# Attention output: the value bank's two halves are summed by TensorE as they are turned back, and VectorE scales the sum

## The reference

```python
# branch A (latent attention), one block of queries
s = jnp.where(mask[None, None], s.astype(jnp.float32), NEG_INF)
p = jax.nn.softmax(s, axis=-1).astype(v_a.dtype)
return jnp.einsum('bhqk,bkhd->bqhd', p, v_a)
# branch B (sparse attention): top-k keys, a bias by distance, then the same softmax and product
p = jax.nn.softmax(s, axis=-1).astype(vs.dtype)
return jnp.einsum('bhqk,bqkhd->bqhd', p, vs)
```

## Time and profile before

| | before |
|---|---|
| median of 3 runs | 1461.71 us (1460.07 to 1461.95) |
| the profiled execution's own time | 1460.28 us |
| its span, first to last instruction | 1458.5 us |
| mean granted TensorE clock | 0.969 |
| PE / PEld busy | 93% / 77% |
| DVE / ACT / POOL busy | 69% / 45% / 31% |

### The profile page before, as it was taken

How to read it: one execution, slowest core, us unless ns; L and a number is a source line. 1 busy time by engine, 2 the same in 40 slices (tenths; PEclk the granted TensorE clock), 3 DMA queues, 4 the chain that set the end, 5 groups by cost and what they waited for, 6 DMA issues and landing times. The chain is left out here.

```text
span 1458.5 us, 21714 instructions
## 1 busy us (share of the span) xinstructions
PE 1361.1 (93%) x7307; PEld 1117.2 (77%) x7308; DVE 1007.6 (69%) x1891; ACT 659.6 (45%) x1175; POOL 459.2 (31%) x497
## 2 busy tenths in 40 slices
PE   6989999999999999999999979999859999999973
PEld 4779888888989978888777768899857776777741
DVE  5448999999970277777777754342387777777746
ACT  5348323321212146777777741121135666666622
POOL 1100335421215545555555214200112332333313
PEclk9999999999999999999999989999959999999996
DMA  6031543257432904868776255222279999999818
GB/s 213 30 143 40 185 161 111 88 197 228 134 101 100 246 1 80 187 134 225 210 206 179 68 178 159 86 89 87 73 281 389 348 366 351 356 379 372 344 58 326
DMA packets 106926, 273.76 MB, mean 188 GB/s; under 512 B 27393, under 2 KB 56737, under 8 KB 94425
## 3 DMA queue, kind: packets, MB, share of 16 engines
q1 hardware_dynamic: 92208, 229.20, 45.5%
q0 software_dynamic: 13584, 38.62, 10.4%
q10 hardware_dynamic: 1048, 4.82, 0.9%
HBM read 246.99 MB, written 85.96 MB: 228 GB/s over the span
## 5 line engine op out<-in xcount | busy, mean ns | idle before, releaser
L445 PE MATMUL ps<-hHi,g_lead 128*128 128x512 f32 (+2 forms) x480 | 184.5, 384 | 5.8 <-DVE hLo L877 3.6
L330 DVE TENSOR_SCALAR_CACHE_REDUCE mask<-score,cand 128x272 bf16<-128x272 f32 (+6 forms) x224 | 185.5, 892 | 4.6 <-DVE cand L349 4.4
L2364 DVE TENSOR_TENSOR w_rest<-wgu,w_lead 128x1024 fp32r<-128x1024 f32 x128 | 156.0, 1222 | 46.4 <-ACT w_lead L2309 45.2
L446 PE MATMUL ps<-hLo,g_lead 128*128 128x512 f32 (+2 forms) x480 | 183.9, 383 | 0.0
L447 PE MATMUL ps<-hHi,g_rest 128*128 128x512 f32 (+2 forms) x480 | 182.6, 380 | 0.0
L1382 DVE TENSOR_TENSOR pL<-ps,pH 128x512 fp32r<-128x512 f32 (+3 forms) x224 | 124.8, 573 | 56.8 <-ACT pH L1321 54.2
L2309 ACT CAST w_lead<-wgu 128x1024 fp32r<-128x1024 f32 x124 | 130.8, 1055 | 48.3 <-PE ps L2252 48.3
L762 POOL TENSOR_TENSOR g_rest<-g_raw,g_lead 128x2048 fp32r<-128x2048 f32 x12 | 56.7, 4722 | 298.4 <-ACT g_lead L619 298.4
L1321 ACT CAST pH<-ps 128x512 fp32r<-128x512 f32 (+3 forms) x224 | 106.0, 495 | 53.8 <-PE ps L1266 53.1
L2250 PE MATMUL ps<-w_lead,x_lead 128*128 128x512 f32 x256 | 114.5, 447 | 4.0 <-DVE x_rest L2371 4.0
L2272 PE MATMUL ps<-wd,hmT 128*128 128x512 f32 x256 | 115.3, 593 | 1.6 <-DVE hmT L2387 1.0
(11 more groups left out here) (382 smaller groups left out, 3414.3 us busy)
## 6 DMA issues: line engine op xcount, KB each, us to landing
wgu<-in_w_exp_gate SPq DMA_DIRECT2D x32, 1024.0 KB
wgu<-in_w_exp_up SPq DMA_DIRECT2D x32, 1024.0 KB
wd<-in_w_exp_down SPq DMA_DIRECT2D x32, 1024.0 KB, 11.8
bias_d<-mask_d POOLq DMA_DIRECT2D x8, 2368.0 KB, 15.6
g_raw<-in_w_in SPq DMA_DIRECT2D x16, 1024.0 KB, 7.2
gates_d<-stage SPq DMA_DIRECT2D x32, 256.0 KB, 2.0
gt<-gates_d SPq DMA_DIRECT2D x32, 256.0 KB, 3.1
tbm<-bias_d SPq DMA_DIRECT2D x8, 976.0 KB, 6.2
```

The source lines that it names most:

```text
L330: return dve.tensor_scalar(mask[:, OFF[i]:OFF[i + 1]], score[:, OFF[i]:OFF[i + 1]], thr, 0.0, op, ALU.add, accum_out=cnt[:, i:i + 1])
L445: pe.matmul(dst, x[0], y[0], start=(k == 0), stop=False)
L446: pe.matmul(dst, x[0], y[1], start=False, stop=False)
L2364: dve.tensor_tensor(w_rest[u][:, :, 2 * part:2 * part + 2, :], wgu[u][:, :, 2 * part:2 * part + 2, :], w_lead[part][:, :, :, :].bitcast(F3 ...
```

## The change

The four transposes of a q turn become four true float32 matmuls. The stationary operand is a block of `oT`, as it was, and the moving operand is a constant `fold` of 128x64: two identity matrices of 64 on top of each other. Each product is therefore 128 tokens by 64, the sum of both halves, and a q turn writes 256 columns of its bank, not 512. DVE's reduction into `otmp` goes; DVE multiplies the bank by `rec` straight into `otok`. POOL's scaling goes, with its place in POOL's order and its waits. `fold` is made once, early on, by one DVE addition of 128x64. The semaphore `s_qa` goes; the bank is free when `s_om` counts.

```diff
+        fold = keep("fold", VD)
@@ early, where the other small constants are made
                 dve.memset(onesb[:, :], 1.0).then_inc(s_cb, 1)
+                dve.tensor_tensor(fold[:, :], ident[:, 0:VD], ident[:, VD:2 * VD], ALU.add).then_inc(s_cb, 1)
@@ TensorE, emptied() and turn()
                     elif kind == "q":
-                        pe.wait_ge(s_qa, s + 1)
+                        pe.wait_ge(s_om, s + 1)
                         elif kind == "q":
-                            mm = pe.transpose(dst, oT[s % 2][:, P * b:P * (b + 1)], ident)
+                            mm = pe.matmul(bank[:, VD * b:VD * (b + 1)], oT[s % 2][:, P * b:P * (b + 1)], fold[:, :],
+                                           start=True, stop=True)
@@ VectorE
                     elif kind == "q":
                         dve.wait_ge(s_t, k + 1)
-                        if s >= 2:
-                            dve.wait_ge(s_om, s - 1)
-                        both = bank_of(k).rearrange("p (b l c) -> p b c l", b=4, l=2)
-                        dve.tensor_reduce(otmp[s % 2][:, :, :], both, AX.X, ALU.add).then_inc(s_qa, 1)
+                        dve.wait_ge(s_rc, s + 1)
+                        if s >= 4:
+                            dve.wait_ge(s_t, turn_of[("o", 4 * (s // 4) - 4 + 2 + s % 2, 0)] + 1)
+                        u, c = s // 2 % 2, 4 * (s % 4)
+                        dve.tensor_tensor(otok[s % 2][:, :].rearrange("p (b c) -> p b c", b=4)[:, :, VD * u:VD * (u + 1)],
+                                          bank_of(k)[:, 0:4 * VD].rearrange("p (b c) -> p b c", b=4),
+                                          rec[:, c:c + 4].unsqueeze(2).to_broadcast([P, 4, VD]),
+                                          ALU.mult).then_inc(s_om, 1)
@@ GpSimd
-                def scaled(s):
-                    ...
-                    if s >= 1:
-                        scaled(s - 1)
                     if s % 2 == 1 and s // 2 + 2 < H:
                         joined(pool, s // 2 + 2)
-                scaled(NSS - 1)
```

More of the change, by code:

```diff
@@ L1049, in hybrid_layer @@
         oT = [at(f"oT{k}", [P, 512], F32, R_X + 4096 * RING + 2048 * k) for k in range(2)]
-        otmp = [at(f"otmp{k}", [P, 4, VD], F32, R_S + 16384 + 1024 * k) for k in range(2)]
         OaT = at("OaT", [P, 4, T], F32, R_W)
@@ L1142, in bank_of @@
             return ps[:, bank_no[k], :]
-        (s_qk, s_ml, s_ex, s_t, s_ld, s_rs, s_pv, s_ot, s_qa, s_rc, s_om, s_oe, s_z, s_vz, s_hl, s_hr, s_vl,
-         s_vr) = map(sem, ["s_qk", "s_ml", "s_ex", "s_t", "s_ld", "s_rs", "s_pv", "s_ot", "s_qa", "s_rc",
+        (s_qk, s_ml, s_ex, s_t, s_ld, s_rs, s_pv, s_ot, s_rc, s_om, s_oe, s_z, s_vz, s_hl, s_hr, s_vl,
+         s_vr) = map(sem, ["s_qk", "s_ml", "s_ex", "s_t", "s_ld", "s_rs", "s_pv", "s_ot", "s_rc",
                            "s_om", "s_oe", "s_z", "s_vz", "s_hs", "s_hr", "s_vl", "s_vr"])
```

## The result

The changed kernel takes 1466.1 us (median of 8 runs, 1463.45 to 1466.75), the kernel before in the same runs 1461.17. The ratio is 1.0032, interval 1.0023 to 1.004: slower by 4.9 us. The same kernel timed again beside the experiments gave 1.0027, 1.0015 to 1.0039.

The account below looks back on a forecast made before the run. Branch A was taken to go at PE's pace, branch B at that of PE, DVE and ACT waiting in turn. TensorE's +5.9 us less 0.5 at the end gave +5.4, 1467.1 us; range 1460.5 to 1473.0.

Parts of the forecast that it names:

- The likeliest case: Whole kernel: longer q turns on TensorE outweigh a shorter stage end, +5.4 us; chance 58%.
- The bound of 2.9 us: Forecast's lower bound, if branch B's turns inside odd steps cost nothing and branch A's even-step ends 0.1 us each.
- A q turn grows by 0.46 us: Attention's q turns on TensorE: eight weight loads at 0.112 us; full price inside branch A's odd steps, 7 turns, 3.2 us.
- The last inner turn: q turn inside the attention stage's last step: put at 0.3 us longer.
- The first rival: q turns on TensorE: the fold goes at the pace of its columns, 4.6 us faster, 1457.1 us; chance 7%.
- Ends of branch A: Seven q turns at even steps' ends in branch A: a wait of PE swallows part, 0.15 us each remains, 1.0 us.
- Ends of branch B: Eight q turns at even steps' ends in branch B: PE's hole of 0.69 us hides the growth, cost nothing.
- Inner turns of branch B: Eight q turns inside branch B's odd steps: four 1.2 us via late ACT work, four 0.2 us after earlier POOL values.
- POOL, nothing but the end: POOL's dropped scaling, 32 x 0.61 us: hardly waited for, worth no more than four value waits and the stage's end.
- The end, -0.5: Last q turn to last o turn: 2.13 us becomes about 1.6, a gain of 0.5 us.
- The second rival: Branch A's holes behind turns inside odd steps swallow more: +1.7 us, 1463.4 us; chance 23%.
- The third: Rival for all 32 q turns: nothing is swallowed, +14.2 us, 1475.9 us; chance 12%.

Follow-up runs that it names:

- reduced fold: The changed kernel with `oT` and `fold` in the reduced-precision float32 format, one matmul and one weight load per product: 1458.71 us, ratio 0.998 against the kernel before.

## Why the prediction was right, point by point

Forecast was +5.4 us and 1467.1, measured 1466.1, +4.9 in the runs and +4.60 in the stage. The likeliest case came true, with its mechanism and for its largest term. Two smaller terms came out too high, by 0.6 and 0.3 us, and the second of them is near the mark only by luck, since two errors of opposite sign lie in it. (The bound of 2.9 us in the forecast doesn't come out of its terms either: 3.2 + 0.7 + 0.3 - 0.5 = 3.7.)

- **A q turn grows by 0.46 us, because loads set 0.112 us.** Right: 0.90 against 0.44, 0.45 over each inner turn of branch A, 3.17 us in all for a forecast of 3.2. The run with 32 columns and the one with half the pairs show that pairs count, and the first two starts of a turn, 0.055 apart, that it is the load. The last inner turn, forecast at 0.3, cost 0.45 too. The first rival, the pace of the columns, is out. The rule behind it in the Trainium skill, page FP8 and Floating Point Precision, section TensorE Precision Notes (four passes for true float32), doesn't give the price here: by the prediction's estimate from it a turn would take 0.43 us, and it took 0.90.
- **Ends of branch A, 1.0 forecast, 0.39 measured.** The step that was mis-sized is the hole: I took 0.36 and 0.27, and it swallowed 0.39 to 0.42 of the 0.46. In the earlier trace rows the transposes behind the hole show 0.66 for four, where four without a wait show 0.60: the first weight load, otherwise hidden behind earlier work, lies bare after a wait. It starts together with its matmul there, at 610.47; in the changed kernel, without a wait, it starts 0.11 before. When the fold fills the hole, these 0.06 us go too: 0.46 - 0.36 - 0.06 = 0.04, as in four of the seven turns. In the other three, at 0.07, the hole is smaller, but the turn grows by less, since a single transpose stands right behind it. One of them, before:

```profile
629.01 0.60 PE L1268 MATMUL ps<-con,oT 128*128 128x128 f32 x4
...
629.73 0.34 PE L1283 MATMUL ps<-pL,VS 128*128 128x384 f32 x1
630.18 0.66 PE L1266 MATMUL ps<-con,pxa 128*128 128x128 f32 x4
```

and in the changed kernel, where the transposes follow without idle time:

```profile
631.74 1.00 PE L1269 MATMUL ps<-fold,oT 128*128 128x64 f32 x8
...
632.87 0.34 PE L1285 MATMUL ps<-pL,VS 128*128 128x384 f32 x1
633.04 0.60 PE L1267 MATMUL ps<-con,pxa 128*128 128x128 f32 x4
```

From the turn's start to the 384-column matmul it was 0.72 us and is now 1.13, 0.41 more; the hole was 630.18 - 629.73 - 0.17 = 0.28, and 0.41 - 0.28 - 0.06 = 0.07.

- **Ends of branch B, nothing.** Right, 0.00; doubling the fold shows that 0.74 us would have fitted in four of them and 1.13 in the others. The 0.74 is the hole of 0.69 and the 0.06 again.
- **Inner turns of branch B, 1.4 forecast, 1.09 measured, for the wrong reasons.** TensorE's part is 2.91 us here, not 1.4 (changed kernel against reduced fold), and DVE's part is -1.8 to -1.9, which I had counted at nothing. The step that failed is the sentence that the reduction is followed by work that waits for PE, now 0.46 later. That was so in the earlier trace rows, but it holds only once PE is late; the pace of the chain before was DVE's, so that DVE's 0.26 comes off first. And I explained four turns by POOL's values, whose waits show; with POOL left as it was these turns were the same. Why PE's 0.46 costs 0.45 in four of the turns and 0.27 in the other four wasn't tried apart from that; the runs only show that it does.
- **POOL, nothing but the end.** Right: -0.02 to +0.19 in each kind of turn without the scaling, and 139.6 us of its waiting were worth 0.7 us. In the changed kernel POOL waits as long elsewhere: 130.9 us for PE, in front of the values.
- **The end, -0.5.** Right: 2.13 to 1.62 us, forecast 1.6. The DVE product was put at 0.42 and took 0.424.
- **The second rival**, holes of branch A behind inner turns that swallow more, is out: 0.45 of 0.46 reach the next turn in each. **The third**, nothing swallowed, is out by the ends of both branches.

## What to carry to other kernels

Moving an addition into TensorE by a true float32 product with a constant costs here by load and matmul pairs, two for each product, whether it has 32 or 64 columns; count pairs against the transposes they replace before counting columns, and look up a pair's price for the format of its weights. An engine's work of a given length has a price only with a place: the same 0.26 us of DVE were worth 0.24 in one kind of turn and nothing in the other four before the end, and 0.61 us of an engine for which nobody waits were worth nothing 31 times of 32. If the pairs can be halved by a cheaper number format, the same fold turns from a loss of 0.3% into a gain of 0.15 to 0.2%: the cost on TensorE goes, and what is left is the shorter work on DVE and the shorter end.

## What the runs showed of the hardware that I had not expected

- A DVE product with both inputs in SBUF took 1.17 to 2.20 us instead of 0.42 when it fell on a subtraction of POOL's, 13 times of 32; read from PSUM it took 0.42 to 0.43 in all 32. The change multiplies straight from PSUM: its product fell on such a subtraction 16 times and took 0.41 to 0.43 us each time. With reduction and product both on DVE and the product reading SBUF, the stage was 10.5 us longer.
- Behind a wait of PE the first transpose of a turn is followed by the next after 0.14 to 0.17 us, without one mostly after 0.11, so a hole is worth up to 0.06 more than its idle time to whoever fills it.
- Seven pairs of weight load and matmul in bf16, with 128x128 weights and 32 columns, started 0.027 us apart at the lower clock level, where float32 pairs started 0.213 apart.
